# A two-layer decoder trunk: x's rounded parts by token tile, an earlier seventh expert load, and a shared product in the last pair

## The reference, cut to what matters

```python
for l in range(DEPTH):                                   # 2 layers, 256 tokens, 1024 columns
    mix = _token_mixer(x, w_in[l], ..., w_out[l])        # three kinds of attention, output product
    x = _layer_norm(ALPHA * x + mix, ln1_g[l], ln1_b[l])
    ffn = _moe(x, w_router[l], b_router[l], w_gate[l], w_up[l], w_down[l],
               ws_gate[l], ws_up[l], ws_down[l])
    x = _layer_norm(ALPHA * x + ffn, ln2_g[l], ln2_b[l])

# _moe: 64 experts, each token takes 8 of them
h = jax.nn.silu(xb @ w_gate[e]) * (xb @ w_up[e])         # 1024 -> 256
return h @ w_down[e]                                     # 256 -> 1024
shared = (jax.nn.silu(xt @ ws_gate) * (xt @ ws_up)) @ ws_down
```

## Time and profile before

| | us |
|---|---|
| median of 3 runs | 1243.32 (1243.03 to 1244.64) |
| the profiled execution | 1243.99 |
| its span, first to last instruction | 1242.20 |
| PE busy | 1211.8 (98%) |
| PE weight loads busy | 632.6 (51%) |
| DVE busy | 554.5 (45%) |
| DMA, mean rate over the span | 366 GB/s |

### The profile page before, as it was taken

One profiled execution on the slowest core, in us unless ns is written; L12 is line 12 of the kernel. 1 busy time (PEld: TensorE's weight loads), 2 busy tenths in 40 slices (PEclk: granted clock), 3 DMA queues, 4 the chain that ended last, 5 costly groups with the idle time before them and its releaser, 6 DMA issues.

```text
span 1242.2 us, 25271 instructions
## 1 busy us (share of the span) xinstructions
PE 1211.8 (98%) x10409; PEld 632.6 (51%) x10411; DVE 554.5 (45%) x1549; ACT 342.9 (28%) x705; POOL 121.7 (10%) x165
## 2 busy tenths in 40 slices
PE   9998999999999999999999989999999999999995
PEld 8885754334444333443389858433433444443341
DVE  5788553333333333333368876433333333333334
ACT  4667321111111111111256574111111111111111
POOL 2661110000000000000035521000000000000000
PEclk9999999999999999999999999999999999999998
DMA  9544699999999999999945538999999999999994
GB/s 358 174 178 196 256 389 426 425 428 426 426 425 426 426 427 426 425 428 425 383 156 200 206 134 352 391 427 425 425 427 426 425 426 426 427 426 425 425 427 196
DMA packets 42425, 454.88 MB, mean 366 GB/s; under 512 B 4944, under 2 KB 5712, under 8 KB 8016
## 3 DMA queue, kind: packets, MB, share of 16 engines
q1 hardware_dynamic: 42032, 452.27, 87.8%
q10 hardware_dynamic: 288, 1.05, 0.2%
HBM read 452.26 MB, written 1.05 MB: 365 GB/s over the span
## 4 chain that ended last, share of the span: by engine, by line
PE 81%; DVE 9%; DMA 5%; ACT 3%; issue 2%; DVEq 0%; ACTq 0%; POOL 0%; POOLq 0%
PE banks L1039 33%; PE banks L1059 17%; PE banks L1015 7%; PE banks L1070 5%; DMA expert_weights<-in_moe_w 5%; ACT prob L1296 2%; PE banks L1047 2%; PE banks L959 1%; PE banks L906 1%; PE banks L907 1%; PE banks L908 1%; PE banks L626 1%; PE banks L594 1%; PE banks L996 1%; PE banks L596 1%
## 5 line engine op out<-in xcount | busy, mean ns | idle before, releaser
L1039 PE MATMUL banks<-expert_weights,gathered 128*64 128x512 f32 x1520 | 339.8, 595 | 1.9 <-DMA expert_weights<-in_moe_w 1.9
L1039 PEld LDWEIGHTS banks<-expert_weights,gathered 128*64 128x64 f32 x1520 | 105.6, 137 | 231.2 <-issue 231.2
L1059 PE MATMUL banks<-expert_weights,hT 128*32 128x512 f32 x1600 | 182.0, 595 | 2.5 <-DVE hT L1872 2.5
L1867 DVE TENSOR_TENSOR sig<-sig,banks 128x256 f32<-128x256 f32 x64 | 26.9, 421 | 339.3 <-ACT sig L1411 339.0
L1424 ACT ACTIVATE y_hi<-banks,gate_slot 128x512 fp32r<-128x512 f32 x126 | 86.6, 687 | 295.1 <-PE banks L1059 295.1
L1877 DVE SCALAR_TENSOR_TENSOR y_lo<-banks,gate_slot,y_hi 128x512 fp32r<-128x512 f32 x126 | 94.6, 751 | 157.6 <-ACT y_hi L1424 157.6
L1411 ACT ACTIVATE sig<-banks 128x256 f32<-128x256 f32 x64 | 24.6, 384 | 408.1 <-PE banks L1039 408.1
L1015 PEld LDWEIGHTS banks<-hot,x_part 128*128 128x128 bf16 x3072 | 93.3, 98 | 48.7 <-issue 48.7
L1059 PEld LDWEIGHTS banks<-expert_weights,hT 128*32 128x32 f32 x1600 | 47.5, 109 | 109.4 <-issue 107.9
L1015 PE MATMUL banks<-hot,x_part 128*128 128x64 bf16 x3072 | 100.6, 193 | 0.0
L1477 POOL TENSOR_TENSOR piece_lo<-piece,piece_hi 128x256 fp32r<-128x256 f32 x112 | 88.0, 824 | 78.9 <-ACT piece_hi L1236 63.3
(11 more groups left out here) (241 smaller groups left out, 1529.5 us busy)
## 6 DMA issues: line engine op xcount, KB each, us to landing
expert_weights<-in_moe_w SPq DMA_DIRECT2D x132, 2048.0 KB, 23.4
expert_weights_in_ring<-in_moe_w SPq DMA_DIRECT2D x20, 2048.0 KB, 23.4
piece<-in_pieces SPq DMA_DIRECT2D x32, 1024.0 KB, 5.0
expert_weights<-in_moe_w SPq DMA_DIRECT2D x26, 1024.0 KB, 8.7
expert_weights_in_rows<-in_moe_w SPq DMA_DIRECT2D x22, 1024.0 KB, 22.7
expert_weights_in_x<-in_moe_w SPq DMA_DIRECT2D x22, 1024.0 KB, 23.4
expert_weights_in_ring<-in_moe_w SPq DMA_DIRECT2D x8, 1024.0 KB, 8.7
shared_weights<-in_ws SPq DMA_DIRECT2D x2, 3072.0 KB, 12.1
```

What stands on the lines that cost most here:

```text
L1039: mm = pe.matmul(C[e * PAIR:(e + 1) * PAIR, :], xgT[:, d, e * PAIR:(e + 1) * PAIR], w[e][:, part], start=(d == 0), stop=(d == KD - 1))
L1059: mm = pe.matmul((A, B)[c][to:to + SLOTS, :], hT[:, f, of_:of_ + SLOTS], W[QUARTERS + c][e][:, f * 512:(f + 1) * 512], start=(f == 0), sto ...
```

## The change

Three things. `x_hi` and `x_lo` become two views of one tensor `x_hi_lo` of shape `[P, TT, 2, KD, P]`: all that belongs to token tile 0 lies in the first 8 KB of a partition, all of tile 1 in the next 8 KB. All readers and writers are rewritten for it; no instruction is added or taken away by that. Load 6 joins `IN_TWO`; its first half (6a), which falls on tile 0's place, is issued at `mix` 2, ahead of the first quarter, and its second half (6b) stands where load 6 stood. And the last of the four shared down products, `shared_down(1, 1)`, leaves pair 21 and goes into the last pair: its first matmul between `add_back` and `turn_h`, its second between `turn_h` and `down`.

```diff
@@ the table of shared products
-             **{SHARED_FROM + 5 + n: ("down", n % 2, n // 2) for n in range(4)}}
+             **{SHARED_FROM + 5 + n: ("down", n % 2, n // 2) for n in range(3)}}
-IN_TWO = [... k in (0, 3, 8, 9, 10, 11, 12, 13, LOADS * PAIRS - 1)]
+IN_TWO = [... k in (0, 3, 6, 8, 9, 10, 11, 12, 13, LOADS * PAIRS - 1)]
@@ placement
-        x_hi = place("x_hi", [P, KD, T], F32R, where=sp_at)
-        x_lo = place("x_lo", [P, KD, T], F32R, where=sp_at)
+        x_parts = place("x_hi_lo", [P, TT, 2, KD, P], F32R, where=sp_at)
+        x_hi, x_lo = x_parts[:, :, 0], x_parts[:, :, 1]
@@ SP
+                    sp.wait_ge(*at(mix, TT))
+                    load_half(6, 0)
                     sp.wait_ge(*at(mix, 2 * TT - 1))
                     load_first_quarter(0)
                     load_half(3, 1)
@@
                     load_first_quarter(1)
                     load(5)
-                    load(6)
+                    load_half(6, 1)
@@ PE, column_products (three_products and out_product: x_hi[:, t, k, :] in the same way)
-                            pe.matmul(out_, hi[:, k, cols], x_hi[:, k, :], ...)
+                            pe.matmul(by_tile(out_), hi[:, k, cols], x_hi[:, :, k, :], ...)
@@ PE, the last pair
-                    def shared_down(t, c):
+                    def shared_down(t, c, fs=range(2)):
                         pe.wait_ge(*at(sh_h, 1))
-                        for f in range(2):
+                        for f in fs:
@@
                         if last:
                             add_back(main, 1 - s, n)
+                            shared_down(1, 1, (0,))
                         turn_h(main, n + 1)
+                        if last:
+                            shared_down(1, 1, (1,))
@@ POOL (ACT and DVE in the same way)
-                        own.link(G.tensor_copy(x_hi[:, o, :], xT[:, o, :]))
-                        G.tensor_tensor(x_lo[:, o, :], xT[:, o, :], x_hi[:, o, :].bitcast(F32), ALU.subtract)...
+                        own.link(G.tensor_copy(x_hi[:, :, o, :], by_tile(xT[:, o, :])))
+                        G.tensor_tensor(x_lo[:, :, o, :], by_tile(xT[:, o, :]), x_hi[:, :, o, :].bitcast(F32), ALU.subtract)...
```

More of the change, by code:

```diff
@@ L67, in room_of @@
     return k % ROOMS if k < LOADS * PAIRS - 1 else 0
-IN_TWO = [k for k in range(LOADS * PAIRS) if room_of(k) == LAST_ROOM or k in (0, 3, 8, 9, 10, 11, 12, 13, LOADS * PAIRS - 1)]
+IN_TWO = [k for k in range(LOADS * PAIRS) if room_of(k) == LAST_ROOM or k in (0, 3, 6, 8, 9, 10, 11, 12, 13, LOADS * PAIRS - 1)]
 ROUTED_SCALE = 2.5
@@ L383, in hi_free, with by_tile, by_step, by_step_of_xT @@
                 eng.wait_ge(*at(proj, 2 * c + 2))
+        def by_tile(t):
+            return t.rearrange("p (t c) -> p t c", t=TT)
+        def by_step(parts, g):
+            return parts[:, :, 4 * g:4 * g + 4, :]
+        def by_step_of_xT(g):
+            return xT[:, 4 * g:4 * g + 4, :].rearrange("p k (t c) -> p t k c", t=TT)
         def flat_piece(t):
@@ L589, in three_products @@
                     def three_products(out_, n, t, ks, opens=True):
-                        cols = slice(t * P, (t + 1) * P)
                         hi, lo = hi_of(n), piece_lo[n % RING]
                         for k in ks:
-                            pe.matmul(out_, x_hi[:, k, cols], hi[:, k, :], start=(k == 0 and opens), stop=False, skip_group_check=True)
-                            pe.matmul(out_, x_hi[:, k, cols], lo[:, k, :], start=False, stop=False, skip_group_check=True)
-                            mm = pe.matmul(out_, x_lo[:, k, cols], hi[:, k, :], start=False, stop=(k == KD - 1), skip_group_check=True)
+                            pe.matmul(out_, x_hi[:, t, k, :], hi[:, k, :], start=(k == 0 and opens), stop=False, skip_group_check=True)
+                            pe.matmul(out_, x_hi[:, t, k, :], lo[:, k, :], start=False, stop=False, skip_group_check=True)
+                            mm = pe.matmul(out_, x_lo[:, t, k, :], hi[:, k, :], start=False, stop=(k == KD - 1), skip_group_check=True)
                         return mm
@@ L603, in column_products @@
                         for k in range(KD):
-                            pe.matmul(out_, hi[:, k, cols], x_hi[:, k, :], start=(k == 0), stop=False, skip_group_check=True)
-                            pe.matmul(out_, lo[:, k, cols], x_hi[:, k, :], start=False, stop=False, skip_group_check=True)
-                            mm = pe.matmul(out_, hi[:, k, cols], x_lo[:, k, :], start=False, stop=(k == KD - 1), skip_group_check=True)
+                            pe.matmul(by_tile(out_), hi[:, k, cols], x_hi[:, :, k, :], start=(k == 0), stop=False, skip_group_check=True)
+                            pe.matmul(by_tile(out_), lo[:, k, cols], x_hi[:, :, k, :], start=False, stop=False, skip_group_check=True)
+                            mm = pe.matmul(by_tile(out_), hi[:, k, cols], x_lo[:, :, k, :], start=False, stop=(k == KD - 1), skip_group_check=True)
                         return mm
@@ L905, in out_product @@
                         for k in ks:
-                            pe.matmul(out_, x_hi[:, k, cols], hi[:, :, k, :], start=(k == 0), stop=False, skip_group_check=True)
-                            pe.matmul(out_, x_hi[:, k, cols], lo[:, :, k, :], start=False, stop=False, skip_group_check=True)
-                            mm = pe.matmul(out_, x_lo[:, k, cols], hi[:, :, k, :], start=False, stop=(k == KD - 1), skip_group_check=True)
+                            pe.matmul(out_, x_hi[:, t, k, :], hi[:, :, k, :], start=(k == 0), stop=False, skip_group_check=True)
+                            pe.matmul(out_, x_hi[:, t, k, :], lo[:, :, k, :], start=False, stop=False, skip_group_check=True)
+                            mm = pe.matmul(out_, x_lo[:, t, k, :], hi[:, :, k, :], start=False, stop=(k == KD - 1), skip_group_check=True)
                         return mm
@@ L1263, in _ @@
                             act.wait_ge(*at(xt_sb, 7 + g, 1))
-                        act.copy(x_hi[:, 4 * g:4 * g + 4, :], xT[:, 4 * g:4 * g + 4, :]).then_inc(xhi_ready, 1)
+                        act.copy(by_step(x_hi, g), by_step_of_xT(g)).then_inc(xhi_ready, 1)
                     if layer == 0:
@@ L1744, in _ @@
                     dve.wait_ge(*at(heads_split, KD - 1))
[L1745 to L1746 removed]
+                    own.link(V.tensor_copy(x_hi[:, :, o, :], by_tile(xT[:, o, :])))
+                    V.tensor_tensor(x_lo[:, :, o, :], by_tile(xT[:, o, :]), x_hi[:, :, o, :].bitcast(F32), ALU.subtract).then_inc(heads_split, 1)
                     def add_sublayer(t, c, sublayer):
```

5 lines of the change are left out of this document (2 added, 3 removed).

## The result

| | before | after |
|---|---|---|
| median of 20 runs, us | 1243.78 | 1246.55 |
| the profiled execution, us | 1243.99 | 1245.18 |
| its span, us | 1242.20 | 1243.4 |

The ratio is 1.0018, with a 95% interval of 1.0012 to 1.0025: 2.2 us slower (1.5 to 3.1). The forecast was +0.6 us, 1243.9, and its range ended at 1245.6.

The account below looks back on a forecast made before the run. Each layer's end was taken as set by the last bytes of the 426 GB/s weight stream, PE a microsecond behind. Tail 0.7 minus gain 0.4, layout zero, over two layers: +0.6 us on 1243.32, 1243.9; range 1241.0 to 1245.6.

Parts of the forecast that it names:

- the new dip: Sign in the early weight stream: the DMA rate would dip between 169 and 176, the first hole having moved there.
- within 0.6 of 179.25: Sign in the early weight stream: half 9a would land within 0.6 us of 179.25, its time before the change.
- 6.6 to 6.8 foretold: Sign in the last pair: down starts 6.6 to 6.8 us after the landing-released gate products, instead of 5.99.
- the rate of 420 from 144 to 149: Sign in the first stream hole: half 6a fills it, so the rate there is near 420 GB/s, 191 before.
- the wait of 2.2 us: Sign at the last gate load: PE, relieved in pair 21, waits about 2.2 us instead of 0.91.
- Part 2, the tail: Last pair: the two moved shared matmuls fill 1.0 us of idle time and cost 0.7 us a layer.
- It is worth nothing: Pair 21: removing two matmuls, 1.72 us on PE, gains nothing, because PE waits at the end anyway.
- Part 1, d = 0.4 us a layer gained: Early weight stream: half 6a early makes half 11b land d = 0.4 us sooner a layer; bounds 0 to 1.3.
- the stream is full from 194 on: Stream after half 11b's landing: no more holes, so the 0.4 us a layer gained passes on to the end.
- Rival A: Early stream: restarting costs only the first landing, 2.5 us a layer gained, -3.6 us in all, 1239.7; chance 0.14.
- Rival B: Last pair: shared matmuls find no idle time, 1.72 us paid a layer, no stream gain, +3.4 us, 1246.8; chance 0.07.
- Rival C: Last pair: idle time hides more, tail costs 0.2 us a layer, 1242.9; chance 0.15 together with the change failing.

Follow-up runs that it names:

- 6a early and 8a late: Layout change with half 6a issued early and half 8a (1 MB) moved right behind it, against the kernel before: 1243.97 us, ratio 1.0008.
- 8a late: The kernel before with half 8a (1 MB) issued behind load 4 instead of some 44 us earlier: 1246.96 us, ratio 1.0022.

## Why the prediction was wrong

The forecast was +0.6, the measurement +2.2 (1.5 to 3.1). Of its signs, the new dip came (257 GB/s from 170 to 175), 9a landed at 178.94, within 0.6 of 179.25, but 0.7 later if both are counted from 8b, and down came 6.85 us after the gate products (6.6 to 6.8 foretold); the rate of 420 from 144 to 149 and the wait of 2.2 us did not come (325 and 0.93). Term by term:

- **Part 2, the tail: right in mechanism, small by 0.16.** "0.7 us a layer", bounds 0.65 and 0.95; measured 0.86 in both layers and again with the product moved alone. I had let PE go on 0.23 to 0.33 us after the start of its last `add_back` row. It was 0.33 (610.46 to 610.79), and the shared matmuls take 0.96 and 0.95 us (610.79 to 611.75, 611.97 to 612.92), not 0.86 as in pair 21; the turning between them takes 0.22 and not 0.32. Over two layers this is 0.3 us of the miss.
- **"It is worth nothing" for pair 21: right**, shown by the kernel without the product. The way I put it was wrong: the wait at load 94 did not grow to 2.2, since PE's lead is waited away at the second gate loads before it, in layer 0 from pair 29 on. This cost the forecast nothing, and two experiments their expectation.
- **Part 1, d = 0.4 us a layer gained: the step that failed.** Right were the mechanism of the first step (the filled hole opens another) and its place (the dip between 168 and 180). Already the steps up to it were too kind: I had 7b land 1.1 us after the issue of 8b, and it landed 2.7 after it (issued at 160.02, 12.1 us to landing; before 3.7), so of 2.6 us of lead only 1.0 was there, since the first hole was not filled but halved; the shared weights, which I had as ended before 145.27, landed at 145.60. And 9a landed 9.5 us after that issue, foretold 8.5, before 8.8. Then I ended the sum at 11b and let "the stream is full from 194 on" do the rest. 11b was 0.3 us earlier counted from 8b; 12a, one DMA later, was 1.4 us later, and the last gate weights 1.1 later in layer 0. In layer 1 they were 0.6 earlier. Half 6a early without the product shows +1.15 and +0.06, and 0.8 of the 1.15 came in at load 94 alone. The third kernel with 6a early, the one with the product ahead of the last gate half, had those weights 0.6 and 0.2 us sooner than before (434.83 for 435.40, 435.38 for 435.54). So the six values of these three traces run from 0.6 sooner to 1.2 later, 0.2 later in the mean. Traces without 6a scatter as much (in layer 1 these weights land 435.1 to 436.2 us after the issue of 8b). The gain of 0.4 a layer is not there in the mean, and a loss is not shown either. The two kernels with and without 6a early differ by 0.0001 in ratio. Put at zero or a little below, in place of 2 x 0.4 gained, d accounts for the larger part of the miss: 1.7 for the tails and 0 to 0.5 for 6a make 1.7 to 2.2.
- **Rival A, the stream keeps its lead**, given 0.14: out. So is the rule that I set beside it. The Trainium skill's "DMA: Bandwidth & Descriptors", section "Anatomy of one DMA", gives a fixed 2.0 us and 2.4 of transfer for 1 MB; by these two figures, an estimate, 8b would have landed at 174.6, 2.4 us behind 7b (172.15). This case's trace has it at 176.46, 4.3 behind 7b and 7.0 after its issue, so the measurement decides against them here.
- **Rival B, slower with the tail at its full 1.72 and d = 0**: not as priced, since 0.86 of the product's 1.72 us was not paid in either layer; but the side was its side. What it asked for, tail minus d above 1.25 a layer, was met by the other term in the profile's layer 0, 0.86 + 1.1, and not in layer 1, 0.86 - 0.6.
- **Rival C, a tail of 0.2 us**: out, it was 0.86.

The prediction called a loss "no change" that 20 runs against 20 could tell, and its range, up to 1245.6, missed the median of 1246.55. 0.46 us of the distance are not of the change: the 3 runs of before lay at 1243.32, the 20 at 1243.78. And the range counted d from nothing upwards, though layer 0 of this profile had -1.1.

**Left open.** Why one half (12a in the changed kernel, 12b with 6a early and 8a late) lands up to 1.7 us behind its turn although the rate has recovered. It is not of 6a alone: in the kernel without the product, which is before up to pair 21, 12b landed 3.7 us behind 12a. The traces give no packet's engine, so they can't say whether one DMA engine lags. Load 94 lagged in the same way by 0.8 to 1.0 us in layer 0 of three traces (6a early, and 8a late twice), which is open too. And how much of the 2.7 us of 8a late is the stream's: its profiles show about 1.

## What to carry to other kernels

Fill a hole in a stream of transfers only if the places that it needs next come free earlier too; here pair 0's products freed them at the same time, and the hole moved 25 us on. In a stage whose end is set by its last transfer, work in the middle can be free, as in pair 21, and cost about half its time anywhere in the last step: before you move it, look for its price in the idle times on both sides of the last landing. What pays at such an end is to make the last landing release as little work as possible, here one load in two halves: 2.2 us.

## What the runs showed of the hardware that was not expected

A queue that is nearly dry lands its next megabytes late even when they were issued in good time: 10a took 7.2 us with 9b still landing in front of it, and 6.9 in the changed kernel, against 5.0 for a megabyte on idle engines in the mixer. Before the change it was issued 2.4 us ahead of 9b's landing and still landed 4.8 behind it. And after such a stretch single halves can land 3.2 to 4.2 us behind the one before in place of 2.46, in the changed kernel while the rate is full again:

```profile
187.00:200.00 13.00, 13.00 (x123) 5.38 (x122) 4.70 (x14) 2.34 (x4) 0.00 (x0) 1.00 1.01 425
```

This row is the window of 187 to 200, in which 12a landed at 196.9.
